# Value products of a step moved behind both heads' turns, in a hybrid decoder trunk on one core

## What is computed

```python
# layer 0, 8 heads, q and k of 96, v of 64: causal, in blocks of 128 queries
s = jnp.einsum('bhqd,bhkd->bhqk', qi, k) * scale
s = jnp.where(kpos[None, :] <= qpos[:, None], s, NEG_INF)
p = jax.nn.softmax(s, axis=-1)
return jnp.einsum('bhqk,bhkd->bhqd', p, v)
...
# layer 1, 16 heads of 64 in 2 groups: three branches, each with its gate
s = jnp.einsum('bqghd,bkgd->bghqk', qi, k_win) * scale      # local: the last 512 keys
s = s + tab[t5_bucket(wdist)].transpose(2, 3, 0, 1)
p_w = jax.nn.softmax(jnp.where(wmask, s, NEG_INF), axis=-1)
o_w = jnp.einsum('bghqk,bkgd->bqghd', p_w, v_win)
...
o = gate[..., 0:1] * o_c + gate[..., 1:2] * o_s + gate[..., 2:3] * o_w
```

## Time and profile before

| | |
|---|---|
| time of three runs | 2578.77, 2580.64 (median), 2590.7 us |
| profiled execution | 2584.01 us, span 2582.2 us |
| TensorE busy | 2500.5 us, 97% of the span, 14136 matmul records |
| DVE, ACT, POOL busy | 69%, 43%, 47% |
| chain that ended last | 83% TensorE, 9% DVE, 3% issue, 2% POOL, 2% ACT |
| latent attention's steps | about 265 to 431 us of the span |
| local part's steps | about 1362 to 1607 us of the span |

### The profile page before, as it was taken

The page is one execution under the profiler, slowest core; times in us unless marked ns, Lnnn a source line. Parts: engine busy times, 40 slices in busy tenths (PEclk is TensorE's granted clock), DMA queues, the critical chain, the costliest instruction groups (busy, mean ns, idle before and its releaser), DMA issues.

```text
span 2582.2 us, 38249 instructions
## 1 busy us (share of the span) xinstructions
PE 2500.5 (97%) x14136; PEld 2009.6 (78%) x14136; DVE 1780.4 (69%) x2851; ACT 1110.8 (43%) x2142; POOL 1203.8 (47%) x935
## 2 busy tenths in 40 slices
PE   7999989999999999999999999999999999999999
PEld 5777666888887778877877777778788888787887
DVE  6554745467778999964037777676646677899993
ACT  4626544243334344323126666566524333433430
POOL 5462677234445444443315777546423444544441
PEclk9999999999999999999999999999999999999999
DMA  4011002223442544303231112353222344264431
GB/s 171 33 50 33 1 1 111 78 90 135 151 163 106 212 155 174 128 33 130 88 96 56 54 54 75 87 144 93 100 89 90 135 151 163 106 216 165 162 127 65
DMA packets 91198, 275.78 MB, mean 107 GB/s; under 512 B 9879, under 2 KB 39191, under 8 KB 76359
## 3 DMA queue, kind: packets, MB, share of 16 engines
q1 hardware_dynamic: 87464, 255.18, 29.0%
q10 hardware_dynamic: 3552, 18.18, 1.8%
HBM read 197.50 MB, written 73.86 MB: 105 GB/s over the span
## 4 chain that ended last, share of the span: by engine, by line
PE 83%; DVE 9%; issue 3%; POOL 2%; ACT 2%; DMA 1%; DVEq 0%; SPq 0%; ACTq 0%; POOLq 0%
PE ps L1710 20%; PE ps L1715 20%; PE ps L1714 20%; PE ps L2275 5%; PE ps L2293 5%; PE ps L2250 2%; DVE RL L922 2%; PE ps L1939 1%; DVE U_lo L956 1%; PE ps L2265 1%; PE ps L2266 1%; PE ps L1966 1%; POOL MX L1514 1%; DVE H L986 1%; DVE H L975 1%
## 5 line engine op out<-in xcount | busy, mean ns | idle before, releaser
L1710 PE MATMUL ps<-U_hi,RH 128*128 128x512 f32 x912 | 357.5, 392 | 13.1 <-DVE H L975 5.6
L1714 PE MATMUL ps<-U_lo,RH 128*128 128x512 f32 x912 | 356.2, 391 | 0.0
L1715 PE MATMUL ps<-U_hi,RL 128*128 128x512 f32 x912 | 356.2, 391 | 0.0
L1110 POOL TENSOR_TENSOR RL<-RAW,RH 128x512 fp32r<-128x512 f32 x112 | 155.1, 1385 | 394.5 <-ACT RH L814 394.5
L814 ACT ACTIVATE RH<-RAW 128x512 fp32r<-128x512 f32 x280 | 175.5, 628 | 289.1 <-PE ps L1715 281.7
L1710 PE MATMUL ps<-U_hi,W_hi 128*128 128x512 f32 (+2 forms) x656 | 261.9, 399 | 13.3 <-DVE U_lo L2987 12.0
L1710 PE MATMUL ps<-SH,RH 128*128 128x512 f32 x656 | 256.0, 390 | 6.3 <-DVE H L975 4.7
L1715 PE MATMUL ps<-U_hi,W_lo 128*128 128x512 f32 (+2 forms) x656 | 258.1, 393 | 0.0
L1714 PE MATMUL ps<-U_lo,W_hi 128*128 128x512 f32 (+2 forms) x656 | 257.9, 393 | 0.0
L1714 PE MATMUL ps<-SL,RH 128*128 128x512 f32 x656 | 255.2, 389 | 0.0
L1715 PE MATMUL ps<-SH,RL 128*128 128x512 f32 x656 | 255.2, 389 | 0.0
(11 more groups left out here) (403 smaller groups left out, 6094.4 us busy)
## 6 DMA issues: line engine op xcount, KB each, us to landing
W_raw<-in_pieces SPq DMA_DIRECT2D x30, 1024.0 KB, 5.3
RAW<-in_pieces SPq DMA_DIRECT2D x28, 1024.0 KB, 4.9
RAW<-in_pieces SPq DMA_DIRECT2D x56, 512.0 KB, 7.7
hid_d<-HOA SPq DMA_DIRECT2D x24, 1024.0 KB, 3.9
hid_d<-HOB SPq DMA_DIRECT2D x24, 768.0 KB, 5.4
RHA<-hid_d SPq DMA_DIRECT2D x12, 1024.0 KB, 5.1
RHB<-hid_d SPq DMA_DIRECT2D x12, 768.0 KB, 6.7
U_rawh<-hid_d SPq DMA_DIRECT2D x12, 768.0 KB, 4.9
```

The lines of the kernel that those rows point to most:

```text
L1110: G_.tensor_tensor(ring(RL[i], n), quarter(n, (B22, B11)[i - 5]), ring(RH[i], n).bitcast(F32), ALU.subtract).then_inc(u_lop.sem, 1)
L1710: m = mm(o, a_hi, b_hi, start=first, stop=False, skip_group_check=again)
L1714: mm(o, a_hi, b_lo, start=False, stop=False, skip_group_check=again)
L1715: return mm(o, a_lo, b_hi, start=False, stop=last, skip_group_check=again)
```

## The change

The value products of step s-1 leave their place between the turns of the two heads of step s and follow both. In the latent attention they so follow the preparation of the next pair too. In the sparse attention it is done for the steps whose products belong to the local part (`0 < s <= N_BR`), and the selected part keeps the order it had. No other engine's program is changed.

```diff
@@ latent attention, TensorE
                 if s < M_STEP:
                     m_turn(2 * s)
-                if s:
-                    m_weigh(s - 1)
-                if s < M_STEP:
                     for pair, j in m_prep_of(s):
                         m_prep(pair, j)
                     m_turn(2 * s + 1)
+                if s:
+                    m_weigh(s - 1)
@@ sparse attention, TensorE
                 if s < N_STEP:
                     turn_p(2 * s)
-                if s:
+                if s > N_BR:
                     weigh_p(s - 1)
                 if s < N_STEP:
                     turn_p(2 * s + 1)
+                if 0 < s <= N_BR:
+                    weigh_p(s - 1)
```

## The result

The changed kernel takes 2602.45 us (median of six runs, 2595.62 to 2607.13) against 2582.82 us before (six runs on the same chip, 2578.23 to 2590.70): the ratio is 1.0082, with a 95% interval of 1.0069 to 1.0095. The two profiled executions lie 17.7 us apart (spans 2582.2 and 2599.9 us). TensorE's busy time hardly moves, 2500.5 us before and 2501.7 after, so the loss is time in which it stands.

| stage, by TensorE's timeline | before, us | after, us | difference |
|---|---|---|---|
| latent part: first scores to first matmul of the output projection | 178.84 | 186.30 | +7.5 |
| from there to the first turn of the local part | 932.06 | 932.26 | +0.2 |
| local part: first turn to the first turn of the selected part | 253.38 | 263.04 | +9.7 |
| from there to the end | 966.05 | 966.44 | +0.4 |

What follows compares the result with a forecast made beforehand. TensorE was taken as the bound (busy 92% in the latent part, 97% in the local). Terms 7.7 + 0.5 + 7.0 = +15.2 us gave 2599.2 for the profiled execution, 2596 us against the median; range 2578 to 2606.

Steps and rivals of the forecast that it cites:

- Local part: Local attention: waits for banks no longer covered by value products, less saved changes of tile shape; +7.7 us.
- +0.5 of step 64: First step of the selected part, with only two banks: it waits for two copies, +0.5 us.
- Per eight steps ... eight times: Local part: 1.01 us lost per eight steps, taken eight times, less 0.43 for step 0, gives +7.7 us.
- +0.32 in plain long steps: Local five-block steps: second head's second chunk waits 0.46 us for ACT's copy, less 0.14 for a saved shape change.
- The sign that the prediction named: Local part: transposes waiting for ACT's PT and DVE's PC, 0.3 to 0.5 us in every second step.
- the bound under which it would have called itself wrong: Waits of the named kinds, in the local and latent parts, under 0.2 us.
- The time from a copy's end to TensorE: Both parts: delay until TensorE sees a freed bank, put at 0.1 us, bounds 0 and 0.3.
- Latent part: Latent attention: uncovered waits for ACT's bank copies and POOL's second normalisation, summed over the pairs of heads; +7.0 us.
- Rival 1: Cover isn't needed, only 64 shape changes of 0.14 us are saved: 9.0 us less, to 2572 us; chance 0.16.
- Rival 2: TensorE's losses shorten its later waits for maxima and POOL, at most 10.4 of 15.2 us: 2585 to 2590; chance 0.20.
- Rival 3: New gaps in the last latent pair lower TensorE's clock, about 2 us each place, 2604 us and over; chance 0.06.
- the low end of that term: Latent part's first pair: its gap and the half clock after it gone, -3 us against the sum.

Runs made afterwards that it cites:

- e3: Against the kernel before: only the local part's value products moved, and ACT copies the first head's first chunk twice in 32 five-block steps; local part 277.06 us for 253.38.
- e2: Against the kernel before: only the local part's value products moved, latent part in the old order; ratio 1.0042 (1.0027 to 1.0057).
- e5: Against the kernel before: value products moved only in the local part's short steps (one chunk a head); ratio 0.9988 (0.9977 to 0.9998).
- e8: Against the kernel before: only the latent part's value products moved, except at each pair's second step; latent part 182.19 us for 178.84.
- e9: Against the kernel before: latent value products moved, and ACT copies the first head's first chunk twice in eight steps of the middle two pairs; latent part 193.04 us for 178.84.
- e1: Against the kernel before: only the latent part's value products moved, local part in the old order; ratio 1.0034 (1.0019 to 1.0049).
- e7: Against the kernel before: value products moved only in the third to last latent step of each of the first three pairs; latent part 180.86 us for 178.84.

## Why the prediction was right

It said 2596.0 us (2578 to 2606), slower with 0.52; measured were 2602.45. Its sum was +15.2 against +17.7 in the profiled executions, so the mechanism held and two terms were too small. The 17.7 depends on which clocks the two profiles were granted: counted at full clock, the parts below give 9.7 + 0.5 + 9.5 = 19.7, near the 19.6 between the medians.

- **Local part, 7.7 forecast, 9.7 measured.** The +0.5 of step 64 came out as +0.53; it lies behind the first turn of the selected part, so it is the +0.4 of the table's last row. In the regular middle of the part (the fourth block of eight steps) the steps changed by +0.63, 0, +0.26, -0.15, +0.40, -0.15, +0.27 and -0.16: 1.10, against +0.43, 0, +0.32, -0.14, +0.36, -0.14, +0.32 and -0.14, 1.01. What the sum missed is three other blocks, the first, second and sixth, which lost 1.66, 1.43 and 1.42: 4.51 us, where it had 0.58 (step 0 has no value products), 1.01 and 1.01. In the first two other users of the three banks are late, or POOL's probabilities are, and turns without a cover meet them; in the first block of the profile after:

```profile
1376.49 0.41 PE L2274 MATMUL ps<-cs,PW 128*128 128x128 f32 x2 [0.86 <-DVE QLM L3365]
...
1380.42 0.74 PE L2274 MATMUL ps<-cs,PW 128*128 128x128 f32 x5 [0.96 <-DVE CKL L3382]
...
1396.38 0.74 PE L2274 MATMUL ps<-cs,PW 128*128 128x128 f32 x5 [0.98 <-POOL PW L1572]
```

In the second block the like waits are for DVE's `KSS` (keys), 0.97 us, and for POOL, 0.42. What makes two long steps of the sixth block dearer (+0.56 and +0.43 for +0.40 and +0.27) is open. The step that failed is "Per eight steps ... eight times": the pattern of the middle was taken for the whole.
- **Which copy.** The prediction put +0.32 in plain long steps on ACT's first chunk, free at 1.45 behind the turn. The size was nearly right (+0.27), but from step 14 on these steps all carry a compressed value product, and the wait that is seen is DVE's `ZQ`, for the bank that the second turn needs first; ACT's bank comes free 0.4 later and is needed 0.44 later, so it adds nothing. The dose in e3 shows that ACT's is the next limit, with next to no slack. That the compressed value product's bank is held was on no line of the sum. The sign that the prediction named, waits for ACT's `PT` of 0.3 to 0.5 us, is in no row of after, and the waits for `ZQ`, 0.2 us each, lie at the bound under which it would have called itself wrong.
- **The time from a copy's end to TensorE**, put at 0.1 us between 0 and 0.3, is two values in the profile after: 0.15 us at all 23 waits for `PC` and `ZQ`, and 0.05 at most of the 20 for ACT's `MT` (median 0.05, longest 0.14).
- **Latent part, +7.0 forecast, +7.5 measured, and this agreement is partly luck.** The first pair lost 1.5 (forecast 1.1). Between profiles at full clock (e2 and after) the second pair lost 2.98 (forecast 2.1) and the last 2.4 (1.7); the third, counted without its half clock, some 2.7 (2.1). That makes 9.5 or 9.6. Before's profile held three stretches at half clock worth 1.7, 1.6 and 0.3 us, after's one of about 1.5, which takes 2.1 off. By steps of the second pair: the two first +0.75 (forecast +0.70), then +0.80 (+0.63), +1.18 (+0.74; +0.90 in the third pair), +0.65 (+0.47), -0.41 (-0.43). The bank came free about when forecast: in the third of these steps the preparation begins 1.35 us behind the turn, in the fifth the second turn 1.44, for 1.38. What the sum left out is that the moved value products begin 0.10 to 0.12 later behind the second turn than the scores did in their place, and that from the scores behind them to the next turn it takes 0.10 more; the sum had no such cost in the latent part, on the ground that the count of shape changes stays. In the fourth step of the second pair ACT's copy starts 0.97 behind the turn, for 0.70 in that of the third pair; why it starts late there is open.
- **Rival 1**, that only changes of shape are saved, holds in the short steps alone (e5).
- **Rival 2**, that waits are given back, happens in small: a pair's first step, which the sum left at nothing, loses 0.56, and the next step, which ends in POOL's wait, takes 0.52 of it back (6.89 us in e8, where its own order is the old one, for 7.41 in e2); the scores' wait for maxima is 3.4 us for 3.9.
- **Rival 3**, the clock: the last pair of after stayed at full speed, and the first pair's gap, now 1.20, did not cost its half clock, the low end of that term. That the risk is real shows in e9: the same last pair, code and gaps as in e1, ran at 0.57 from 420 to 424 us, and that step took 9.88 us for 8.26.

## What to carry to other kernels

A group of matmuls that waits for nothing can be the cover under which other engines empty the banks that the next group needs; before moving it, compare its length with the time from the last use of each bank to its release, step by step, the irregular first steps too. A wait that doesn't show in the profile of before can be found by its sum: turn, copy, latency, arrival. A dose of the suspected delay, once in each order, tells cover from coincidence better than the whole change does.

## What was not expected of the hardware

The granted clock after a gap of one length is not the same from run to run: 1.96 and 1.97 us before the same matmuls gave full clock in one profile and 0.56 in another. So stages were compared by steps at full clock, and a difference of 3 us between two profiles of the latent part proves nothing by itself. Of the stretch between the two attentions, same code throughout, profiles showed 926.8 us (e1) to 932.7 (e8), and from the selected part to the end 966.1 (before) to 971.9 (e7); the cause was not looked into.
